# Feed-forward norms applied after the product: raw rows turned, gains by column, row scale by a table

## Reference

```
def rms_norm(x, g):
    return x * rsqrt(mean(x * x, axis=-1) + 1e-6) * g

# end of the first block
x = x + moe(rms_norm(x, g_ffn), ...)          # top 4 of 32 experts
gate = sigmoid(rms_norm(x, g_ple) @ w_ple_gate)
x = x + (p @ w_ple_proj) * gate
x = rms_norm(x, g_final)

# second block, for each of two layers
x = x + 0.5 * swiglu(rms_norm(x, ffa_norm), ffa_w_in, ffa_w_out)   # inner width 2816
h = rms_norm(x, mix_norm)
... three mixers, gates ...
x = x + mixed @ w_out
x = x + 0.5 * swiglu(rms_norm(x, ffb_norm), ffb_w_in, ffb_w_out)
```

## Time and profile before

| | |
|---|---|
| median of 3 runs | 2455.78 us (2453.0 to 2456.02) |
| profiled execution, its own time | 2455.39 us |
| its span | 2453.6 us |
| PE, DVE, ACT, POOL busy | 99%, 37%, 36%, 41% |
| experts (PE's loop) | about 110 to 1027 us |
| PLE | 1027 to 1075 us |
| layer 0, layer 1 | 1075 to 1767, 1767 to 2453 us |

### The profile page before, as it was taken

How to read it: one execution, slowest core, us unless ns; L and a number is a source line. 1 busy time by engine, 2 the same in 40 slices (tenths; PEclk the granted TensorE clock), 3 DMA queues, 4 the chain that set the end, 5 groups by cost and what they waited for, 6 DMA issues and landing times.

```text
span 2453.6 us, 34874 instructions
## 1 busy us (share of the span) xinstructions
PE 2419.6 (99%) x13863; PEld 1713.7 (70%) x13863; DVE 920.0 (37%) x1736; ACT 888.6 (36%) x1457; POOL 1013.1 (41%) x430
## 2 busy tenths in 40 slices
PE   8999999999999999999999999999999999999999
PEld 6744444444444444468889899888888898998887
DVE  5622222222222222262248764332432388653322
ACT  6411111101111110154457624544444477425443
POOL 0000000000000000048877436788788785546886
PEclk9999999999999999999999999999999999999999
DMA  8799999999999999935555224465555553334654
GB/s 291 291 427 429 429 430 429 430 430 429 430 429 431 429 430 429 413 102 197 189 164 180 95 96 145 161 203 190 166 198 189 166 184 112 121 100 150 202 186 144
DMA packets 96584, 653.07 MB, mean 266 GB/s; under 512 B 10864, under 2 KB 13336, under 8 KB 69848
## 3 DMA queue, kind: packets, MB, share of 16 engines
...
## 4 chain that ended last, share of the span: by engine, by line
PE 88%; DMA 8%; DVE 2%; ACT 1%; issue 1%; POOL 0%; SPq 0%; DVEq 0%; ACTq 0%
PE bank L2256 22%; PE bank L831 13%; PE bank L631 10%; PE bank L633 10%; PE bank L632 10%; PE bank L832 7%; DMA ring<-in_expert_units 4%; PE bank L2243 4%; DMA scratch<-in_expert_units 4%; PE bank L1226 3%; PE bank L2264 2%; PE bank L2272 1%; PE bank L1104 1%; PE bank L1075 1%; PE bank L1182 0%
## 5 line engine op out<-in xcount | busy, mean ns | idle before, releaser
L618 POOL TENSOR_TENSOR w_lo<-raw,w_hi 128x1024 fp32r<-128x1024 f32 (+2 forms) x424 | 1009.2, 2408 | 1198.2 <-ACT w_hi L612 1198.2
L2256 PE MATMUL bank<-ring,scratch 128*64 128x512 f32 x2304 | 513.4, 596 | 8.6 <-DMA ring<-in_expert_units 8.6
L831 PE MATMUL bank<-hT_both,w_hi 128*128 128x512 f32 x1408 | 498.3, 398 | 1.7 <-DVE hT_both L722 1.7
L612 ACT CAST w_hi<-raw 128x1024 fp32r<-128x1024 f32 (+2 forms) x424 | 422.3, 1042 | 169.1 <-PE bank L633 155.5
L832 PE MATMUL bank<-hT_both,w_lo 128*128 128x256 f32 x1408 | 395.9, 281 | 0.0
L2256 PEld LDWEIGHTS bank<-ring,scratch 128*64 128x64 f32 x2304 | 160.0, 137 | 323.2 <-issue 318.3
L831 PEld LDWEIGHTS bank<-hT_both,w_hi 128*128 128x128 f32 x1408 | 265.1, 188 | 67.6 <-issue 3.4
L2489 DVE TENSOR_TENSOR scratch<-bank,scratch 128x512 f32<-128x512 f32 x64 | 44.3, 692 | 594.8 <-PE bank L2272 590.7
L832 PEld LDWEIGHTS bank<-hT_both,w_lo 128*128 128x128 f32 x1408 | 266.7, 189 | 0.6
L909 DVE TENSOR_REDUCE scratch<-bank 128x256 f32<-128x512 f32 x88 | 60.8, 691 | 358.4 <-PE bank L832 358.4
L2256 PE MATMUL bank<-scratch 128*64 128x512 f32 x768 | 172.1, 596 | 2.2 <-DMA scratch<-in_expert_units 2.1
...
## 6 DMA issues: line engine op xcount, KB each, us to landing
ring<-in_expert_units SPq DMA_DIRECT2D x144, 2048.0 KB, 25.0
...
scratch<-in_expert_units SPq DMA_DIRECT2D x47, 2048.0 KB, 25.9
ring<-in_first_units SPq DMA_DIRECT2D x11, 1024.0 KB, 10.0
ring<-in_ple_units SPq DMA_DIRECT2D x2, 2048.0 KB, 18.6
...
```

The costliest lines, as they stand in the source:

```text
L612: k.nc.scalar.copy(k.w[0][i % SPLIT_SLOTS][:, at], k.raw[n % RAW_SLOTS][:, 0:at.stop - at.start]).then_inc(k.shared("weights_hi"), 1)
L618: k.nc.gpsimd.tensor_tensor(k.w[1][i % SPLIT_SLOTS][:, at], k.raw[n % RAW_SLOTS][:, 0:at.stop - at.start], k.w[0][i % SPLIT_SLOTS][:, at], ...
L831: nc.tensor.matmul(bank[:, :], w[0], both, start=start, stop=False)
L2256: last = nc.tensor.matmul(b[g * SL:(g + 1) * SL, :], lhsT[:, c, :], w[:, c, g, :], start=start and c == 0, stop=stop and c == 3)
```

## The change

- Ahead of both feed-forward blocks (n = 0 and 2) PE turns x itself. DVE multiplies the turned bank in PSUM by the gains, one per partition and chunk (`lnorm_gained`), then the parts are written as before. Norm 1 is unchanged. The gains come as columns in `fvec`.
- Sums of squares, variance and root are taken beside that. `diag_dve` writes the identity times the row scale; PE multiplies it by ones (`rstd_pe`), which gives a table of 128x256 with the row scales along the columns; DVE copies it and multiplies each gate bank (512) and each sum of up (256) by it.
- `rstd_pe` stands between the first and second half of (1, 0). Unit 0 runs its column halves outermost; unit 1 uses the banks of the out products. In layer 1 and all second blocks the bank sets are 1, 5, 2, 6 and 0, 3, 4, 7.
- Transposes move into the products ahead: into the last out-unit of layer 0, into `wout` and into the PLE gate products; the last one into unit 0. Fillers before the first block of layer 0 and before the second blocks go; six stay in layer 1.
- `wout` awaits its last two weight halves one by one. In `ffn_act`, unit 0 calls `past` for both its halves ahead of its first silu.
- The rope tables, and in layer 0 the final scaling of x, move behind (2,0), (2,1), (3,0) and (3,1) of the first block.
- The expert loop of PE runs one group less, and the last group stands behind it as code of its own, without the last turn's gathers.

```diff
+    junk = k.h[:, t, at] if n == 1 else k.s(JUNK + 512 * (2 * t + half), 512)
+    k.nc.scalar.activation(junk, k.x[:, t, at], ACT.Square, accum_out=st[:, 2 * t + half:2 * t + half + 1])\
         .then_inc(k.sem("ss_ready"), 1)
...
+    if n != 1:
+        act.wait_ge(*k.at("turned_gained", 2 * n + LATE_ORDER.index((t, half)) + 1))
...
+def lnorm_gained(k, dve, n, t, half, gain):
+    b, _free = k.filled(dve, ("norm", n, t, half))
+    turned = part(b, 4, P)
+    k.nc.vector.tensor_tensor(turned, turned, bc(gain[:, 4 * half:4 * half + 4].unsqueeze(2), [P, 4, P]), ALU.mult)\
+        .then_inc(k.sem("turned_gained"), 1)
+def diag_dve(k, dve, n, scales):
+    for t in range(NT):
+        dve.wait_ge(*k.at("norm_rstd", 4 * n + t + 1))
+        last = k.nc.vector.tensor_scalar(k.s(RSTD_DIAG, NT, P)[:, t, :], k.c("ident"), scales[t], None, ALU.mult)
+    last.then_inc(k.sem("diag_ready"), 1)
+def rstd_pe(k, pe, n):
+    b, full = k.claim(pe, ("rstd", n))
+    pe.wait_ge(*k.at("diag_ready", n + 1))
+    for t in range(NT):
+        last = k.nc.tensor.matmul(b[:, t * P:(t + 1) * P], k.c("ones"), k.s(RSTD_DIAG, NT, P)[:, t, :], start=(t == 0), stop=(t == NT - 1))
+    last.then_inc(full, 1)
...
-def spare_pe(k, pe):
-    pe.wait_ge(k.shared("weights_split"), 4)
-    b, n = k.uses.at["norm", 0, 1, 0]
-    pe.wait_ge(k.bank_free[b], n)
-    for j in range(20):
-        k.nc.tensor.matmul(k.bank[b][:, :], k.w[0][0][:, j * 64:j * 64 + P], k.w[0][1][:, 512 * (j % 4):512 * (j % 4) + 512],
-                           start=(j == 0), stop=(j == 19))
...
+def x_written(k, eng, n, t, half):
+    if n == 2:
+        k.evacuated(eng, ("wout", t, half))
+        return
+    before, written = (k.part - 1, ("ffn_out", 1, t, half)) if k.part else ("ple", ("proj", half, t))
+    with k.inside(before):
+        k.evacuated(eng, written)
+def lnorm_pe(k, pe, n, t, halves=(0, 1)):
+    rows = k.h if n == 1 else k.x
+    for half in halves:
+        if n == 1:
+            pe.wait_ge(*k.at("h_ready", 2 * t + half + 1))
+        else:
+            x_written(k, pe, n, t, half)
         b, full = k.claim(pe, ("norm", n, t, half))
         for j in range(4):
             c = 4 * half + j
-            last = k.nc.tensor.transpose(b[:, j * P:(j + 1) * P], k.h[:, t, c * P:(c + 1) * P], k.c("ident"))
+            last = k.nc.tensor.transpose(b[:, j * P:(j + 1) * P], rows[:, t, c * P:(c + 1) * P], k.c("ident"))
         last.then_inc(full, 1)
...
+def late_norm_act(k, act, n, x_ready, between):
     def square(t, half):
         x_ready(t, half)
         lnorm_square(k, act, n, t, half)
     square(0, 0)
+    lnorm_hi(k, act, n, 0, 0)
+    square(1, 0)
+    lnorm_hi(k, act, n, 1, 0)
+    between()
     square(0, 1)
-    if n == 1:
...
+    lnorm_root(k, act, n, 0)
+    lnorm_root(k, act, n, 1)
...
+def late_norm_dve(k, dve, link, n, evacuate):
+    gain = k.norm_columns(n)
     evacuate(0, 0)
+    evacuate(1, 0)
+    dve.wait_ge(*k.at("gain_loaded", 16))
+    lnorm_gained(k, dve, n, 0, 0, gain)
     evacuate(0, 1)
-    evacuate(1, 0)
-    lnorm_variance(k, dve, link, n, 0)
-    if last_first:
-        evacuate(1, 1)
-        lnorm_h(k, dve, n, 0, 0)
-        lnorm_variance(k, dve, link, n, 1)
-        lnorm_h(k, dve, n, 0, 1)
-        done = 0
-    else:
-        lnorm_h(k, dve, n, 0, 0)
-        lnorm_h(k, dve, n, 0, 1)
-        evacuate(1, 1)
...
+        banks = out_banks if u == 1 else unit_banks
         for j in range(2):
-            uses.add(("gate", n, u, j), 2 * j)
-            uses.add(("up", n, u, j), 2 * j + 1)
+            if (u, j) == (1, 1):
+                uses.add(("rstd", n), banks[2])
+            uses.add(("gate", n, u, j), banks[2 * j])
+            uses.add(("up", n, u, j), banks[2 * j + 1])
     for t in range(NT):
...
+def ffn_first_pe(k, pe, n):
+    def last_turned():
+        lnorm_pe(k, pe, 2 * n, 1, (1,))
+    opened = {}
+    for h, j in ((0, 0), (0, 1), (1, 0), (1, 1)):
+        if h == 0:
+            opened[j] = ffn_in_banks(k, pe, n, 0, j)
+        if j == 0:
+            hT_written(k, pe, 2 * n, (h,))
+        ffn_in_block_pe(k, n, *opened[j], h, last_turned if h + j == 0 else None)
...
+            if (u, j, h) == (1, 0, 1):
+                rstd_pe(k, pe, n)
+            ffn_in_block_pe(k, n, banks, w, h)
...
+        for at, (t, v) in enumerate(HI_ORDER if between is None else LATE_ORDER):
+            for i in range(2):
+                if between is not None and i == 1 and at >= 2:
+                    between(at - 2)
+                last = product(w, 4 * u + i, i, t, v)
+            last.then_inc(out[t, v][1], 1)
...
+        if u == 0:
+            for j in range(2):
+                splits.past((f"ffn{n}", kind, u, j))
...
+    silu, rstd = k.s(SILU_TMP, 2, S), k.s(RSTD_ROWS, S)
+    b, free = k.filled(dve, ("rstd", n))
+    V_.tensor_copy(rstd, b[:, 0:S]).then_inc(free, 1)
+    k.evacuated(dve, ("rstd", n))
     for kind, u in FFN_STEPS:
         if kind == "out":
             continue
         for j in range(2):
             at = 2 * (FFN_IN_UNITS * n + u) + j + 1
             gate, free = k.filled(dve, ("gate", n, u, j))
+            parts = part(gate, 2, S)
+            link(V_.tensor_tensor(parts, parts, bc(rstd.unsqueeze(1), [P, 2, S]), ALU.mult))
             both_added(k, silu[:, j, :], gate).then_inc(k.sem("gate_sum"), 1)
+            b, up_free = k.filled(dve, ("up", n, u, j))
             dve.wait_ge(*k.at("gate_sum", at))
-            b, up_free = k.filled(dve, ("up", n, u, j))
             both_added(k, gate[:, 0:S], b).then_inc(up_free, 1)
             k.evacuated(dve, ("up", n, u, j))
+            link(V_.tensor_tensor(gate[:, 0:S], gate[:, 0:S], rstd, ALU.mult))
             dve.wait_ge(*k.at("silu", at))
             V_.tensor_tensor(gate[:, 0:S], silu[:, j, :], gate[:, 0:S], ALU.mult).then_inc(k.sem("product"), 1)
             dve.wait_ge(*k.at("act_hi", at))
             hi, lo = (a[:, 2 * u % 12 + j, :] for a in k.act2)
             V_.tensor_tensor(lo, gate[:, 0:S], hi, ALU.subtract).then_inc(free, 1)
+            if u >= 2 and 2 * (u - 2) + j < len(between):
+                between[2 * (u - 2) + j]()
...
+            if h == 1 and c == 2:
+                between(t, v)
             last = mm3(nc, banks[t, v][0][:, :], [a[:, 4 * h + c, t * P:(t + 1) * P] for a in k.hT2], [a[:, c, :] for a in w],
                        start=(h == 0 and c == 0), stop=(h == 1 and c == 3))
...
-    w = [weights_pe(k, pe, ("wout", v, 1), 512) for v in range(2)]
-    for t in range(NT):
-        for v in range(2):
-            product(w[v], 1, t, v).then_inc(banks[t, v][1], 1)
+    for v in range(2):
+        w = weights_pe(k, pe, ("wout", v, 1), 512)
+        for t in range(NT):
+            product(w, 1, t, v).then_inc(banks[t, v][1], 1)
...
+            def gather_next(half):
+                b, full = turn_claim(pe, ("gather", half), it)
+                if final:
+                    pe.sem_inc(full, 1)
+                else:
+                    gather_turn(b, half).then_inc(full, 1)
+            def turn_selection():
                 pe.wait_ge(*k.at("gsel_ready", it + 1))
                 b, full = turn_claim(pe, ("selT",), it)
                 selection_turned(b).then_inc(full, 1)
-                b, full = turn_claim(pe, ("y",), it)
-                pe.wait_ge(*k.at("act_ready", it * 2 + 1))
-                product(4, group, turn, b, acts[:, 0:4, :], True, False).then_inc(k.sem("first_unit_read"), 1)
-                pe.wait_ge(*k.at("act_ready", it * 2 + 2))
-                product(5, group, turn, b, acts[:, 4:8, :], False, True).then_inc(full, 1)
+            pe.wait_ge(*k.at("sel_ready", it + 2))
+            if final:
+                turn_selection()
+                gather_next(0)
+                transposed(1, it)
+                gather_next(1)
+            else:
+                gather_next(0)
+                transposed(1, it)
+                gather_next(1)
+                turn_selection()
+            b, full = turn_claim(pe, ("y",), it)
+            pe.wait_ge(*k.at("act_ready", it * 2 + 1))
+            product(4, group, turn, b, acts[:, 0:4, :], True, False).then_inc(k.sem("first_unit_read"), 1)
+            pe.wait_ge(*k.at("act_ready", it * 2 + 2))
+            product(5, group, turn, b, acts[:, 4:8, :], False, True).then_inc(full, 1)
+        with pe.Fori(0, last) as group:
+            for turn in range(GROUP):
+                turn_pe(group, turn, False)
+        for turn in range(GROUP):
+            turn_pe(last, turn, turn == GROUP - 1)
         for key in (("gather", 0), ("gather", 1), ("selT",)):
-            turn_evacuated(pe, key, turns)
+            turn_evacuated(pe, key, last_turn + 1)
         with k.inside("ple"):
             pe.wait_ge(*k.at("proj_arrived", 16))
             pe.wait_ge(*k.at("p_loaded", 16))
...
+        if t == 1 and c == 6 - v:
+            with k.inside(0):
+                lnorm_pe(k, pe, 0, v, (0,))
...
+    ple_squares_act(k, act, 0, 0)
```

(55 more changed lines are left out.)

318 lines of the change are left out of this document (144 added, 174 removed).

## The result

The changed kernel takes 2464.23 us (median of 6 runs, 2461.92 to 2467.33), the kernel before 2455.36 us on the same chip (6 runs). The ratio is 1.0035, with a 95% interval of 1.0024 to 1.0045: 0.35% slower, where 0.2% can be told from no change. The prediction, 2459.3 (2445 to 2468), had 0.44 on "same" and 0.38 on "slower", so what came is the less likely of the two; the time lies in its range, 4.9 us above its value. The profiled execution took 2463.14 us, with a span of 2461.4 against 2453.6 before.

What follows compares the result with a forecast made beforehand. It took TensorE, busy 99% of the span partly with fillers, to lose time where it turns normalised rows. Gains of 27.1 us against costs of 31.0 made 3.9 slower: 2455.39 + 3.9 = 2459.3 us, range 2445 to 2468.

Steps and rivals of the forecast that it cites:

- PLE start, and its half clock: After the per-layer embedding gate: first feed-forward matmul (t0) 8.8 us earlier, and 1.8 us of half clock gone.
- expert loop: Last turn's useless gathers dropped, so the down product starts near 1017.7: gain 1.7 us (0 to 3.7).
- fourth bank, waits for x and hT, variance: Feed-forward blocks: fourth bank's transposes 1.6, waits for x columns or hT's second half 1.3, PLE variance chains 0.5 us.
- stall ahead of (2,1): PE waits for POOL's weights ahead of unit 2's second half, 4.2 us in each of four blocks: 16.8 us.
- clock after it: Half clock after each stall ahead of (2,1), 1.8 us each: 7.2 us (0 to 8).
- One of the signs: What would show it: first feed-forward matmuls about 9 us after the gate products before, now 1.2.
- DVE may begin only when the table is there: Stall's chain: DVE waits for the row-scale table in unit 1 and starts (0,0) at t0 + 15.25.
- DVE work moved behind (2,0) to (3,1): Moved rope tables and x's scaling delay casts in first blocks: 1.0 us layer 1, 1.6 layer 0; 2.6 (0 to 6).
- "locked out": Rival, 9%: moved two-SBUF-input DVE operations wait a POOL piece several times over in each layer's first block; 2472 us.
- the weights did not come in time: Rival, 12%, that weights for (2,1) come in time: neither stall nor half clock; 2435.3 us.
- the clock did fall: Rival, 15%, that the stall comes but the clock stays full: 2452.1 us.
- hT was not late: Rival, 9%, that ACT or DVE bring hT later, losing half of the 24 us of earlier start: 2471 us.

Runs made afterwards that it cites:

- Experiments 1: Changed kernel with ScalarE's casts of weights one half further ahead behind the first blocks of a feed-forward block: 2450.29 us, ratio 0.9975 to the kernel before.
- 3: Changed kernel without DVE's two multiplications by the row-scale table per (u,j), table still made and awaited: 2441.11 us, ratio 0.9929 to the kernel before.
- 4: Kernel before, with DVE's two extra multiplications per (u,j) added, by ones, waiting for no table: 2455.63 us, ratio 1.0000.
- 7: Changed kernel with one line moved: PE makes the row-scale table ahead of (1,0), not in its middle: 2448.74 us, ratio 0.9974 to the kernel before.
- experiment 6: Changed kernel, DVE multiplying by ones from unit 0; unused real table made ahead of (1,0), copied behind (0,0): 2455.27 us, ratio 0.9999 to the kernel before.
- experiment 2: Changed kernel with sixteen filler matmuls ahead of (2,1)'s wait in all four feed-forward blocks: 2461.38 us, ratio 1.0022 to the kernel before.

## Why the prediction was right or wrong, by its steps

| term | predicted | measured |
| --- | --- | --- |
| PLE start, and its half clock | 8.8 and 1.8 | 8.7 and 1.6 |
| layer boundary | 4.8 | 4.8 |
| `wout`, twice | 10.0 | 4.5 + 5.05 = 9.6 |
| expert loop | 1.7 | 2.0 |
| fourth bank, waits for x and hT, variance | 3.4 | 3.1 |
| table matmuls | 1.0 | 1.6 |
| stall ahead of (2,1) | 16.8 | 15.7 |
| clock after it | 7.2 | 8.3 |
| DVE tables | 2.6 | 5.3 |
| net | +3.9 | +7.3, and 0.4 in no term |

- **The gains** are right in place and size. They are read as differences of t0 and of the stretches in the table above (10.7 for the first t0, of which 2.0 belong to the loop: the last down product ends at 1025.03 and not 1027.02). The 8.7 of the PLE repeat: from that end to t0 PE takes 48.3 us in both executions without the change and 39.5 in all twelve with it. No run takes a single one of the gains back, so they are read from traces and not tested one by one. The low clock is read from the first block before, where (0,0) lasted 7.19 us against 5.55 for its neighbours. One of the signs is misread: the gate products ended 9.97 us ahead of the first feed-forward matmul before (1065.33 to 1075.30), not about 9. The loop's end in PE's timeline after:

```profile
1016.07 0.63 PE L2381 MATMUL bank<-const,scratch 128*128 128x128 f32 x4 [0.41 <-ACT scratch L2479]
1017.78 7.31 PE L2365 MATMUL bank<-scratch 128*64 128x512 f32 x32 [1.08 <-DVE scratch L2618]
```

  The down product starts 2.2 us sooner than in the earlier trace rows, at the 1017.7 that was worked out, and ends 2.0 sooner. Of these, 0.35 are a last expert unit that landed sooner in this execution (1021.31, before 1021.65); from that landing to the end it is 5.37 us before and 3.72 after, 1.65 less, as the forecast of 1.7 had it.
- **The small costs in the block**: (0,0) lasts 1.26, 0.65, 0.52 and 0.65 us longer than its neighbours, 3.1 in all, and (1,0), with the table matmuls, 0.45, 0.35, 0.45 and 0.35. Of the 34.4 us that the blocks cost (32.8 and the 1.6 of low clock that went), 0.4 are in no term of the table; with them the net is 7.7.
- **The stall** is right as a mechanism and to the step: each event of its chain in layer 1 lies within 0.3 us of the working. It is 1.1 us smaller in all: PE asks at t0 + 28.9 to 30.1, not 28.4, and is back at t0 + 32.8 to 33.8, not 32.6. Experiments 1, 3, 4 and 7 bear it out: it goes when the cast is called sooner, nearly when the work goes, and shrinks with an earlier start. Incomplete was the step "DVE may begin only when the table is there": ACT's early casts and table load hold the first silu to t0 + 15.3 as well (experiment 6), so taking away the table alone would not have removed it.
- **The clock** is right in kind (experiment 2: fillers keep it at 1.00) and 1.1 us low in size. That this cancels the 1.1 us of the stall is luck. That its removal saves only 2.8 of 7.8 us was not in the working, which took it as a sum of its own.
- **The failed step** is "DVE work moved behind (2,0) to (3,1)": of the 3.8 us by which the net is off, 2.7 are here. The forecast gave 1.0 to layer 1 and 1.6 to layer 0; it was 5.3 and nothing. It priced one lock for the first tables, 5.1, and followed it to (3,1)'s cast and PE's (4,0). But layer 1 has no scaling of x, so its tables stand behind (2,0) and (2,1), where DVE is latest and POOL has no gap, and both groups pay, 7.4 and 5.6 us, ahead of (3,0)'s cast, which the first down product needs sooner than (4,0). In layer 0 the first group met an idle POOL and cost 1.0. The remaining 1.1 us are spread over the small terms. The "locked out" rival, at 9%, had this mechanism: it added two more pieces and a half clock, 6.6, to each layer's first block. Layer 1 took 4.3 more than the forecast, layer 0 1.6 less, so its size was right in neither.
- **The other rivals**: the weights did not come in time; the clock did fall, four times of four; hT was not late.
